# The samples' w_out tile in two passes, the samples' reads in two column groups, and another order of VectorE and loads behind the last head

## The chip, the cores and the metric

One core of one Trainium2 chip runs the program. The metric is the device time of one execution in microseconds, here the median of three runs: 1043.18 us (1041.35 to 1046.11).

## What is computed

One layer of a hybrid decoder for 1024 prompt tokens and 8 sample tokens (one new token for each of 8 sequences that have a past), with a final norm. Cut to what matters:

```python
def layer(x, ...):                       # x: prompt (1, 1024, 1024), samples (8, 1, 1024)
    z = rmsnorm(x, g_mix) @ w_in         # u | q | k | v | gate_a | gate_b
    pool_out, new_hist = pool_mixer(u, hist, ...)
    ret, s_new = retention(rotary(q), rotary(k), v, s0)     # 4 heads, 128 x 256 state
    mixed = sigmoid(ga) * pool_out + sigmoid(gb) * head_group_norm(ret, ret_gn)
    x = x + mixed @ w_out                # 1024 x 1024
    h2 = rmsnorm(x, g_ffn)
    x = x + hier_moe(h2, w_grp, w_exp, w1, w3, w2)          # 4 groups of 8 experts, top 2
    return x, new_hist, s_new
y = rmsnorm(x, g_final)                  # prompt and samples
```

For a sample, retention is one step for each head: the state is scaled and gets the outer product of key and value, and the query reads it.

## The kernel before

The work runs in stages: norm and transposition of x; four heads; stage C (w_out, second norm, router); the experts; the final norm. Every engine has its own program and they meet at counting semaphores (S["name"]). Each engine does its instructions in the written order, so that a wait holds up all that is written behind it.

**Precision.** Products with weights are made from a rounded part (hi) and the rest (lo) of both operands: hi by hi, hi by lo, lo by hi, in three passes. ScalarE writes hi, VectorE writes lo. The samples' projection in the heads puts hi and lo of the 8 tokens in different columns of one operand (hs) and takes two passes, one for each half of the weight; the partial results land in different rows and are added.

**Heads.** head(h) on TensorE makes nine products for u, q and k (n = 0 to 8, L1836), and between them the samples' part of the head before (attend_samples, L1775): grow(g) forms key by value for two samples, VectorE's update(h, g) (L2067) adds it to the states, read(g) (L1785) multiplies them with the queries. qm holds a query in one column of 32, a different one for each sample, so that all eight products add up in rows 96 to 127 (Q3:P) of one bank. Then follow eight chunks of 128 tokens and the samples as ninth (c = 8): project (v and gates), before (L1863: key transposed, scores of the next chunk), attend. VectorE's finish and finish_rest (L2032, L2053) normalise a chunk's output by head, with Newton steps for the root; GpSimd adds the pool part (L2248), raises sum_done and stores the rows to mixed_d. For the samples of head h-1 they run inside head h behind its products 6 and 7 (L2119, L2122). Behind these come the rotations of q and k, the pool means and scores(0), which writes scm.

**Last head into stage C.** In head 3 the raw w_out is split into hi and lo (low_wout for row blocks 0 to 2, low_wout_rest(i) for blocks 3, 4, 5 and then 6 with 7). TensorE mixes the samples' rest of head 3 with tile 0 of w_out (L947 to L958). VectorE's order is at L2196 to L2208 and L2217 to L2223, and below.

**Stage C.** Nine tiles t, eight of 128 tokens and the samples as tile 8 (CH). SyncE loads mixed rows and x (load_mixed, load_x); mixed_over(t) transposes them, high_mixed and low_mixed split them, out_product(t, ks) makes 48 products of 512 columns in row blocks k = 0 to 7. add_x(t) adds x. Within tile t the rest of tile t-1 is interleaved on TensorE: x2_over (transposes), router, count. VectorE does x2_second_half, norm, picks (group and experts of each token), places (slots in the experts' lists) for it. The loop is L959 to L976 on TensorE and L1201 to L1212 on VectorE. wo_used releases the first expert weights, which lie where w_out was.

```python
            dve.wait_ge(S["on_ready"], after(9 * H))
            dve.tensor_copy(count_b[:, :, :].rearrange("p a n -> p (a n)"), misc[:, BEFORE:BEFORE + 2 * P])
            for t in range(NT):
                if t == 1:
                    fold_router()
                if t > 0:
                    x2_second_half(t - 1)
                if t < CH:
                    low_mixed(dve, t + 1)
                if t > 0:
                    norm(t - 1)
                    picks(t - 1)
                    places(t - 1)
                add_x(t)
```

**SyncE.** tail(h, between) stores and loads the samples' states with other loads between (first_loads_c for the last head); behind its end stands head_stored, and then stage_c_sp, which begins with the four loads for the router (g_ffn in two forms, w_grp, w_exp) behind the last sum_done.

## Time and profile before

| | us |
|---|---|
| median of three runs | 1043.18 (1041.35 to 1046.11) |
| profiled execution, its own time | 1042.78 |
| its span, first to last instruction | 1041.0 |
| TensorE busy | 976.8 |
| VectorE busy | 737.1 |
| ScalarE busy | 443.0 |
| GpSimd busy | 219.0 |
| mean granted clock of TensorE | 0.978 |

PE is TensorE (PEld its loads of the stationary operand, which overlap with it), DVE VectorE, ACT ScalarE, POOL GpSimd, SP SyncE. Times in the rows are microseconds from the start of the span.
### The profile page before, as it was taken

The numbers are of one execution on the slowest core, as the hardware profiler recorded it, in microseconds if no ns is written. First come the engines' busy times: TensorE is split into PE (matmuls) and PEld (weight loads), VectorE is DVE, ScalarE is ACT, GpSimd is POOL, SyncE is SP. The second block draws the span as 40 slices with busy tenths as digits, with TensorE's granted clock in tenths as the row PEclk, the third lists the DMA queues.
The fourth block names the chain that finished last, engine by engine and source line by source line (L and its number), as shares of the span: only waits on it lengthen the run. The fifth ranks groups of instructions, "written<-read, shape, count | busy, mean of one in ns | idle before, by whom it ended". The sixth has DMA issues, their size and how long they took to land.

```text
span 1041.0 us, 16456 instructions
## 1 busy us (share of the span) xinstructions
PE 976.8 (94%) x5342; PEld 842.6 (81%) x5343; DVE 737.1 (71%) x1616; ACT 443.0 (43%) x738; POOL 219.0 (21%) x223
## 2 busy tenths in 40 slices
PE   5899999999999999999997999979999999999980
PEld 4898888988889888898885888857888888888860
DVE  4874556845558555684557555669999999999965
ACT  6622122121220121301112221136898889888974
POOL 0001220012200122011221000012444344443320
PEclk9999999999999999999999999989999999999995
DMA  9511115111151110511215433269999999999938
GB/s 290 195 31 62 31 32 170 31 62 31 32 160 42 30 62 22 173 38 42 71 56 207 170 147 123 103 245 376 388 395 399 390 392 395 394 392 384 361 55 331
DMA packets 74726, 190.23 MB, mean 183 GB/s; under 512 B 12503, under 2 KB 47555, under 8 KB 62227
## 3 DMA queue, kind: packets, MB, share of 16 engines
q1 hardware_dynamic: 61403, 159.66, 40.9%
q0 software_dynamic: 13248, 29.62, 9.8%
q8 instruction: 41, 0.67, 0.3%
q14 instruction: 34, 0.28, 0.1%
HBM read 167.43 MB, written 38.68 MB: 198 GB/s over the span
## 4 chain that ended last, share of the span: by engine, by line
PE 86%; DVE 5%; DMA 5%; issue 2%; ACT 1%; SPq 1%; POOL 0%; DVEq 0%; POOLq 0%; ACTq 0%
PE bank L1909 17%; PE bank L861 12%; PE bank L863 12%; PE bank L862 12%; PE bank L1910 9%; PE bank L892 9%; PE bank L1009 3%; PE bank L1898 1%; PE bank L922 1%; PE bank L1932 1%; PE bank L1924 1%; PE bank L1920 1%; PE bank L1789 1%; DMA raw<-in_w_in_dram 1%; PE bank L1928 1%
## 5 line engine op out<-in xcount | busy, mean ns | idle before, releaser
L1266 DVE TENSOR_TENSOR w_lo<-w,w_hi 128x1024 fp32r<-128x1024 f32 x128 | 150.5, 1217 | 0.2 <-DVE vec L1228 0.2
L750 ACT ACTIVATE w_hi<-w 128x1024 fp32r<-128x1024 f32 x128 | 129.7, 1068 | 3.0 <-PE bank L863 2.9
L1909 PE MATMUL bank<-wvg_hi,hT_hi 128*128 128x512 f32 x256 | 104.3, 407 | 0.0
L861 PE MATMUL bank<-w_hi,xT_hi 128*128 128x512 f32 x256 | 102.8, 402 | 1.3 <-issue 1.3
L1909 PE MATMUL bank<-wvg_lo,hT_hi 128*128 128x512 f32 x256 | 101.0, 395 | 0.0
L1909 PE MATMUL bank<-wvg_hi,hT_lo 128*128 128x512 f32 x256 | 100.7, 393 | 0.0
L863 PE MATMUL bank<-w_hi,xT_lo 128*128 128x512 f32 x256 | 100.2, 391 | 0.0
L862 PE MATMUL bank<-w_lo,xT_hi 128*128 128x512 f32 x256 | 99.8, 390 | 0.0
L1731 ACT ACTIVATE v<-bank 128x256 f32<-128x256 f32 x32 | 12.3, 383 | 201.2 <-PE bank L1910 201.2
L861 PE MATMUL bank<-hT_hi,wuqk_hi 128*128 128x344 f32 x288 | 95.6, 332 | 2.1 <-ACT line L1690 2.1
L2248 POOL TENSOR_TENSOR mixed<-onorm,pgate 128x256 f32<-128x256 f32 x36 | 39.2, 1088 | 276.0 <-DVE onorm L2065 276.0
L863 PE MATMUL bank<-hT_hi,wuqk_lo 128*128 128x344 f32 x288 | 93.3, 324 | 0.0
L862 PE MATMUL bank<-hT_lo,wuqk_hi 128*128 128x344 f32 x288 | 93.3, 324 | 0.0
L2165 DVE SCALAR_TENSOR_TENSOR state<-state,small,bank 128x256 f32<-128x256 f32 x28 | 13.5, 481 | 108.8 <-PE bank L1932 108.7
L1271 DVE TENSOR_TENSOR w_lo<-w,w_hi 128x1024 fp32r<-128x1024 f32 x62 | 73.2, 1222 | 15.7 <-ACT w_hi L758 15.7
L1448 POOL DMA_INDIRECT sum_d<-y,icol x28 | 45.5, 1624 | 133.3 <-ACT y L787 119.8
L1910 PE MATMUL bank<-wvg_hi,hT_hi 128*128 128x256 f32 x256 | 71.8, 280 | 0.0
L1910 PE MATMUL bank<-wvg_lo,hT_hi 128*128 128x256 f32 x256 | 71.7, 280 | 0.0
L1910 PE MATMUL bank<-wvg_hi,hT_lo 128*128 128x256 f32 x256 | 71.7, 280 | 0.0
L2237 POOL TENSOR_TENSOR sg<-sg,gn_b 128x256 f32<-128x256 f32 x36 | 26.6, 740 | 182.1 <-ACT sg L1733 178.2
L758 ACT ACTIVATE w_hi<-w 128x1024 fp32r<-128x1024 f32 x62 | 62.5, 1067 | 0.0
L861 PEld LDWEIGHTS bank<-hT_hi,wuqk_hi 128*128 128x128 f32 x288 | 55.2, 192 | 5.7 <-ACT line L1690 2.5
(262 smaller groups left out, 2388.4 us busy)
## 6 DMA issues: line engine op xcount, KB each, us to landing
w<-in_w_dram SPq DMA_DIRECT2D x96, 1024.0 KB, 17.4
raw<-in_w_in_dram SPq DMA_DIRECT2D x60, 256.0 KB, 3.2
xall<-in_x_prompt_dram SPq DMA_DIRECT2D x8, 512.0 KB, 7.9
mixed_d<-mixed POOLq DMA_DIRECT2D x32, 128.0 KB, 3.3
sample_state<-in_state_ret_dram SPq DMA_DIRECT2D x16, 256.0 KB, 3.6
out_dram<-sample_state SPq DMA_DIRECT2D x16, 256.0 KB, 4.0
mixed_in<-mixed_d SPq DMA_DIRECT2D x8, 512.0 KB, 4.3
x_again<-in_x_prompt_dram SPq DMA_DIRECT2D x8, 512.0 KB, 3.4
```

The costliest lines, as they stand in the source:

```text
L750: act.activation(hi, whole_w, ACT.Copy).then_inc(S["up_hi"], 1)
L758: act.activation(hi, whole_w, ACT.Copy).then_inc(S["down_hi"], 1)
L861: pe.matmul(out, lhs[0], rhs[0], start=first, stop=False)
L862: pe.matmul(out, lhs[0], rhs[1], start=False, stop=False)
L863: return pe.matmul(out, lhs[1], rhs[0], start=False, stop=last)
L892: mm = pe.matmul(banks[4 - 2 * s + n][:, :], mT[s][xi][:, k, :], wo[k][wi][:, n * 512:(n + 1) * 512], start=(k == 0 and xi + wi == 0), sto ...
L1266: dve.tensor_tensor(lo, whole_w, hi, ALU.subtract).then_inc(S["up_lo"], 1)
L1271: dve.tensor_tensor(lo, whole_w, hi, ALU.subtract).then_inc(S["down_lo"], 1)
L1448: pool.indirect_dma_start(out=sum_d, out_offset=bass.IndirectOffsetOnAxis(ap=index, axis=0), in_=yb[s2][:, :], in_offset=None, bounds_chec ...
L1909: g = pe.matmul(gates, x[xi], wvg[wi][:, 1:3, k, :], start=first, stop=last)
L1910: m = pe.matmul(v[:, 0:DV], x[xi], wvg[wi][:, 0, k, :], start=first, stop=last)
L2248: pool.tensor_tensor(mixed[s][:, :], onorm[:, :], pgate[:, :], ALU.add).then_inc(S["sum_done"], 1)
```

## The change

Samples' tile: sample_product takes its place. mT[0][0] holds hi in columns 0 to 7 and lo in columns 32 to 39 (low_samples), the products run with both halves of w_out, 32 in all, first for both halves of the 1024 output columns up to k = 4, then half 0 alone, then half 1. add_x_samples adds x and both row groups, half by half. Reads: the second product of each read goes to rows 64 to 95, and finish for the samples copies them and adds them to rows 96 to 127 before it goes on; finish_rest reads the sum from SBUF. VectorE: low_mixed(0), low_wout_rest(3), low_mixed(1) and add_x(0) stand earlier, finish and finish_rest for the last head's samples later, with waits for sum_done and head_stored behind them; places(0) and count(0) move into tile 2, places(7) behind add_x_samples. SyncE: the four router loads stand in the last head's tail, behind skv_mm. The transposition of gffn8 stands later in tile 1 and waits for pg_ready.

```diff
--- before.py
+++ after.py
@@ -403,7 +403,7 @@
 
         by_pe = {n: sem(n) for n in (
             "xt_mm", "g_col_mm", "uqk_mm", "g_mm", "v_mm", "kt_mm", "sc_mm", "o_mm", "kv_mm", "skv_mm", "so_mm",
-            "ht_mm", "ut_mm", "ct_mm", "w_mm", "wo_used", "t2_mm", "gf_mm", "l_mm", "count_mm", "list_mm",
+            "ht_mm", "ut_mm", "ct_mm", "w_mm", "w_half_mm", "wo_used", "t2_mm", "gf_mm", "l_mm", "count_mm", "list_mm",
             "spill_mm", "xt2_mm",
             "at_mm", "up_used", "down_used")}
         by_act = {n: sem(n) for n in (
@@ -637,16 +637,19 @@
                 load_x(sp, 0)
                 load_mixed(sp, 1)
             elif i == 3:
+                router_loads(sp)
                 load_mixed(sp, 2)
                 load_x(sp, 1)
 
-        def stage_c_sp(sp):
-            sp.wait_ge(S["sum_done"], after(9 * H))
+        def router_loads(sp):
+            sp.wait_ge(S["skv_mm"], after(4 * H))
             sp.dma_start(gffn_b[:, :], g_ffn[0:1, :].to_broadcast([P, D])).then_inc(route_in, 16)
             sp.dma_start(wr[:, :, 0:4], w_grp[0].rearrange("(k p) g -> p k g", p=P)).then_inc(route_in, 16)
             sp.dma_start(wr[:, :, 4:36], w_exp[0].rearrange("(k p) g e -> p k (g e)", p=P))\
                 .then_inc(route_in, 16)
             sp.dma_start(gffn8[0:KT, :], g_ffn[0].rearrange("(k p) -> k p", p=P)).then_inc(route_in, 16)
+
+        def stage_c_sp(sp):
             for t in range(2, CH + 1):
                 if t < CH:
                     load_mixed(sp, t + 1)
@@ -718,6 +721,8 @@
             def x2_first_half(t):
                 act.wait_ge(S["t2_mm"], after(2 * t + 1))
                 act.wait_ge(S["l_mm"], after(t - 1))
+                if t == 0:
+                    act.wait_ge(S["sgn_done"], after(9 * H))
                 m = columns(t)
                 act.activation(h2T[t % 2][:, 0:4, 0:m], banks[6][:, 0:4 * m].rearrange("p (k n) -> p k n", k=4), ACT.Copy)\
                     .then_inc(S["h2a_ev"], 1)
@@ -892,10 +897,20 @@
                             mm = pe.matmul(banks[4 - 2 * s + n][:, :], mT[s][xi][:, k, :],
                                            wo[k][wi][:, n * 512:(n + 1) * 512], start=(k == 0 and xi + wi == 0),
                                            stop=(k == KT - 1 and xi == 1))
-                    if t == CH and k in (2, 5):
-                        mm.then_inc(S["wo_used"], 1)
                 if ks[-1] == KT - 1:
                     mm.then_inc(S["w_mm"], 1)
+
+            def sample_product(ks, halves):
+
+                if ks[0] == 0:
+                    pe.wait_ge(S["m_lo"], after(2 * CH + 2))
+                    pe.wait_ge(S["x2_done"], after(2 * (CH - 1)))
+                for k in ks:
+                    for wi in range(2):
+                        for n in halves:
+                            mm = pe.matmul(banks[4 + n][:, :], mT[0][0][:, k, :], wo[k][wi][:, n * 512:(n + 1) * 512],
+                                           start=(k == 0 and wi == 0), stop=(k == KT - 1 and wi == 1))
+                return mm
 
             def x2_over(t, b):
 
@@ -956,24 +971,37 @@
             last_samples(5)
             last_samples(6)
             out_product(0, range(7, KT))
-            for t in range(1, NT):
-                if t < CH:
-                    mixed_over(pe, t + 1)
+            for t in range(1, CH):
+                mixed_over(pe, t + 1)
                 out_product(t, range(0, 1))
+                if t == 2:
+                    count(0)
                 x2_over(t - 1, 0)
+                out_product(t, range(1, 2))
+                x2_over(t - 1, 1)
                 if t == 1:
                     pe.wait_ge(route_in, 64)
+                    pe.wait_ge(S["pg_ready"], after(9 * H))
                     pe.transpose(banks[7][:, 0:KT], gffn8[0:KT, :], ident[0:KT, 0:KT]).then_inc(S["gf_mm"], 1)
-                out_product(t, range(1, 2))
-                x2_over(t - 1, 1)
                 out_product(t, range(2, 3))
                 router(t - 1)
                 out_product(t, range(3, 7))
-                count(t - 1)
-                if t == CH:
-                    for u in range(CH - 1):
-                        listing(u)
+                if t > 1:
+                    count(t - 1)
                 out_product(t, range(7, 8))
+            sample_product(range(0, 1), (0, 1))
+            x2_over(CH - 1, 0)
+            sample_product(range(1, 2), (0, 1))
+            x2_over(CH - 1, 1)
+            sample_product(range(2, 3), (0, 1)).then_inc(S["wo_used"], 1)
+            router(CH - 1)
+            sample_product(range(3, 5), (0, 1))
+            sample_product(range(5, KT), (0,)).then_inc(S["w_half_mm"], 1)
+            sample_product(range(5, 6), (1,)).then_inc(S["wo_used"], 1)
+            count(CH - 1)
+            for u in range(CH - 1):
+                listing(u)
+            sample_product(range(6, KT), (1,)).then_inc(S["w_mm"], 1)
             x2_over(CH, 0)
             x2_over(CH, 1)
             listing(CH - 1)
@@ -1091,7 +1119,16 @@
                                   mT[s][0][at].rearrange("p k n -> p (k n)"), ALU.subtract)\
                     .then_inc(S["m_lo"], 1)
 
-        def stage_c_dve(dve):
+        def low_samples(dve):
+
+            for b in range(2):
+                dve.wait_ge(S["m_hi"], after(2 * CH + b + 1))
+                own = mT[0][0][:, 4 * b:4 * b + 4, :]
+                turned_b = turned_mixed(CH, b).rearrange("p (k n) -> p k n", k=4)
+                dve.tensor_tensor(own[:, :, 32:32 + NB], turned_b[:, :, 0:NB], own[:, :, 0:NB], ALU.subtract)\
+                    .then_inc(S["m_lo"], 1)
+
+        def stage_c_dve(dve, finish_samples, finish_samples_rest):
             steps = Steps(dve, steps_c)
             do = steps.do
             rev4 = misc[:, REV + 4:REV + 8]
@@ -1196,20 +1233,44 @@
                     dve.tensor_tensor(x2[:, t, half], banks[4 - 2 * s + n][:, :], xr[s][:, half], ALU.add)\
                         .then_inc(S["x2_done"], 1)
 
-            dve.wait_ge(S["on_ready"], after(9 * H))
-            dve.tensor_copy(count_b[:, :, :].rearrange("p a n -> p (a n)"), misc[:, BEFORE:BEFORE + 2 * P])
-            for t in range(NT):
+            def add_x_samples(n):
+
+                dve.wait_ge(S["w_half_mm"] if n == 0 else S["w_mm"], after(1 if n == 0 else NT))
+                dve.wait_ge(xr_in[0], 16 * (CH // 2 + 1))
+                half = slice(n * 512, (n + 1) * 512)
+                do(dve.tensor_tensor(x2[:, CH, half], banks[4 + n][:, :], xr[0][:, half], ALU.add))
+                dve.tensor_tensor(x2[0:NB, CH, half], banks[4 + n][32:32 + NB, :], x2[0:NB, CH, half], ALU.add)\
+                    .then_inc(S["x2_done"], 1)
+
+            low_mixed(dve, 1)
+            add_x(0)
+            finish_samples()
+            for t in range(1, NT):
                 if t == 1:
                     fold_router()
-                if t > 0:
-                    x2_second_half(t - 1)
+                elif t == 2:
+                    places(0)
+                x2_second_half(t - 1)
+                if t == 1:
+                    finish_samples_rest()
+                    dve.wait_ge(S["on_ready"], after(9 * H))
+                    dve.wait_ge(S["sum_done"], after(9 * H))
+                    dve.wait_ge(S["head_stored"], after(H))
+                    dve.tensor_copy(count_b[:, :, :].rearrange("p a n -> p (a n)"), misc[:, BEFORE:BEFORE + 2 * P])
+                if t < CH - 1:
+                    low_mixed(dve, t + 1)
+                elif t < CH:
+                    low_samples(dve)
+                norm(t - 1)
+                picks(t - 1)
                 if t < CH:
-                    low_mixed(dve, t + 1)
-                if t > 0:
-                    norm(t - 1)
-                    picks(t - 1)
+                    if t > 1:
+                        places(t - 1)
+                    add_x(t)
+                else:
+                    add_x_samples(0)
+                    add_x_samples(1)
                     places(t - 1)
-                add_x(t)
             x2_second_half(CH)
             norm(CH)
             picks(CH)
@@ -1772,6 +1833,9 @@
                             if t % 3 == 2 if g < 2 else t == 7:
                                 mm.then_inc(S["xt_mm"], 1)
 
+            def quarter(i):
+                return slice(Q3, P) if i == 0 else slice(64, Q3)
+
             def attend_samples(h, n):
 
 
@@ -1786,8 +1850,8 @@
                     pe.wait_ge(S["s_upd"], after(4 * h + g + 1))
                     for i in range(2):
                         b = 2 * g + i
-                        mm = pe.matmul(sample_bank(h)[Q3:P, 0:DV], qm[:, b, :], sst[g % 2][:, i, :],
-                                       start=(b == 0), stop=(b == NB - 1))
+                        mm = pe.matmul(sample_bank(h)[quarter(i), 0:DV], qm[:, b, :], sst[g % 2][:, i, :],
+                                       start=(g == 0), stop=(g == NB // 2 - 1))
                     mm.then_inc(S["so_mm"], 1)
 
                 if n == 1:
@@ -2027,7 +2091,7 @@
                 elif n > 2:
                     for q in ((7, 8, 9), (10, 11, 12, 13, 14, 15), (16, 17))[n - 3]:
                         low_first(q)
-            per_head, per_tail = 104, 5 + NEWTON
+            per_head, per_tail = 106, 7 + NEWTON
 
             def finish(h, c):
 
@@ -2041,6 +2105,12 @@
                 dve.wait_ge(S["sum_done"], after(9 * h + c))
                 bank = banks[6] if c < CH else sample_bank(h)
                 o = bank[r, 0:DV]
+                if c == CH:
+                    steps.do(dve.tensor_copy(onorm[r, :], bank[64:Q3, 0:DV]))
+                    carried(dve, "dve")
+                    steps.do(dve.tensor_tensor(onorm[r, :], o, onorm[r, :], ALU.add))
+                    carried(dve, "dve")
+                    o = onorm[r, :]
                 dve.tensor_tensor(pgate[r, :], bank[r, DV:2 * DV], sg[s][r, 0:DV], ALU.mult)\
                     .then_inc(S["pg_ready"], 1)
                 steps.do(dve.bn_stats(small[r, STAT:STAT + 6], o))
@@ -2054,7 +2124,7 @@
 
                 r = slice(0 if c < CH else Q3, P)
                 s = c % 2
-                o = (banks[6] if c < CH else sample_bank(h))[r, 0:DV]
+                o = banks[6][r, 0:DV] if c < CH else onorm[r, :]
                 newton_rsqrt(steps, dve, small[r, HALF:HALF + 1], small[r, GUESS:GUESS + 1],
                              small[r, TMP:TMP + 1]).then_inc(S["rstd_done"], 1)
                 dve.wait_ge(S["rstd_done"], after(9 * h + c + 1))
@@ -2189,6 +2259,8 @@
                         dve.wait_ge(S["v_ev"], after(9 * h + 9))
                         dve.tensor_tensor(vs[0:32, :], banks[2][64:Q3, 0:DV], vs[64:Q3, :], ALU.subtract)\
                             .then_inc(S["kblk_done"], 1)
+                        if last:
+                            low_mixed(dve, 0)
                         dve.wait_ge(S["g_mm"], after(9 * h + 9))
                         steps.do(dve.tensor_copy(sg[0][Q3:P, :], banks[1][64:Q3, :]))
                         dve.tensor_tensor(sg[0][Q3:P, :], sg[0][Q3:P, :], banks[1][Q3:P, :], ALU.add)\
@@ -2196,7 +2268,6 @@
                     if c > 0:
                         grow_state(c - 1)
                         if c == CH and last:
-                            low_mixed(dve, 0)
                             sample_queries()
                             update(h, 0)
                             update(h, 1)
@@ -2215,12 +2286,10 @@
             steps.round_(before_heads - per_tail, H, per_head)
 
             low_wout_rest(dve, 2)
+            low_wout_rest(dve, 3)
             update(H - 1, 2)
             update(H - 1, 3)
-            low_wout_rest(dve, 3)
-            finish(H - 1, CH)
-            finish_rest(H - 1, CH)
-            stage_c_dve(dve)
+            stage_c_dve(dve, lambda: finish(H - 1, CH), lambda: finish_rest(H - 1, CH))
 
 
         @block.gpsimd
```

## Rows read from the trace of the kernel before

**Rows 1.** Page: span, busy time by engine, and who ends the chain.

```profile
span 1041.0 us, 16456 instructions
...
PE 976.8 (94%) x5342; PEld 842.6 (81%) x5343; DVE 737.1 (71%) x1616; ACT 443.0 (43%) x738; POOL 219.0 (21%) x223
...
PE 86%; DVE 5%; DMA 5%; issue 2%; ACT 1%; SPq 1%; POOL 0%; DVEq 0%; POOLq 0%; ACTq 0%
```

**Rows 2.** Waits of TensorE: who waited for whom, total, times, longest (us).

```profile
PE bank L876 <- DVE mT_lo L1090: 4.1, 1, 4.1
...
PE bank L892 <- issue: 1.4, 1, 1.4
```

**Rows 3.** Timeline of TensorE: start, us, line, operation, tiles, idle time before.

```profile
548.00 0.70 PE L892 MATMUL bank<-wo_hi,mT_hi 128*128 128x512 f32 x2 [1.44 <-issue]
...
558.24 1.03 PE L876 MATMUL bank<-misc,mixed_in 128*128 128x128 f32 x8
...
562.69 1.91 PE L1789 MATMUL bank<-sample_state,qm 128*32 128x256 f32 x8
...
570.28 1.40 PE L876 MATMUL bank<-misc,mixed_in 128*128 128x128 f32 x8 [4.07 <-DVE mT_lo L1090]
...
587.47 1.03 PE L876 MATMUL bank<-misc,mixed_in 128*128 128x128 f32 x8
...
602.19 1.03 PE L876 MATMUL bank<-misc,mixed_in 128*128 128x128 f32 x8
```

**Rows 4.** Windows: span, busy of PE, PEld, DVE, ACT, POOL, clock, DMA, GB/s.

```profile
572.00:574.00 2.00, 2.00 (x6) 1.46 (x5) 0.00 (x0) 0.00 (x0) 0.00 (x0) 0.50 1.00 203
```

**Rows 5.** Timeline of VectorE, 525 to 720, behind the last head's projection.

```profile
544.77 0.69 DVE L2193 COPY sg<-bank 32x512 f32<-32x512 f32 x1
...
546.62 1.28 DVE L1090 TENSOR_TENSOR mT_lo<-bank,mT_hi 128x512 fp32r<-128x512 f32 x2
...
556.10 1.22 DVE L495 TENSOR_TENSOR wo_lo<-wo_raw,wo_hi 128x1024 fp32r<-128x1024 f32 x1
558.47 1.45 DVE L2070 SCALAR_TENSOR_TENSOR sample_state<-sample_state,small,bank 128x512 f32<-128x512 f32 x2 [1.16 <-DMA sample_state<-in_state_ret_dram]
...
564.64 0.43 DVE L2044 TENSOR_TENSOR pgate<-bank,sg 32x256 f32<-32x256 f32 x1 [2.46 <-PE bank L1789]
```

**Rows 6.** Timeline of ScalarE, 536 to 600: high half of tile 0's operand.

```profile
544.31 1.09 ACT L714 ACTIVATE mT_hi<-bank 128x512 fp32r<-128x512 f32 x2
```

**Rows 7.** Timeline of the SyncE queue, 535 to 760: router loads and tile 3.

```profile
570.26 0.35 SPq L645 DMA_DIRECT2D gffn_b<-in_g_ffn_dram  x1
...
573.52 0.54 SPq L614 DMA_DIRECT2D mixed_in<-mixed_d  x1
```

**Rows 8.** Tile mixed_in, window 573.4 to 574.1: landing of that one load (us).

```profile
DMA to landing us min/median/max: 3.7/3.7/3.7
```

**Rows 9.** Source view of line 1789, the reads: duration in ns min/median/max.

```profile
L1789 PEld LDWEIGHTS bank<-sample_state,qm x64: 106/110/110, 164.4 to 564.0; 128*32 128x32 f32 x64
L1789 PE MATMUL bank<-sample_state,qm x64: 379/379/403, 164.6 to 564.2; 128*32 128x256 f32 x64
```

**Rows 10.** Timeline of VectorE in heads 1 (first two rows) and 3.

```profile
188.32 0.18 DVE L2048 BATCH_NORM_AGGREGATE small<-small 32x2 f32<-32x6 f32 x1 [0.16 <-DVE small L2046]
...
205.26 0.29 DVE L2130 TENSOR_TENSOR scm<-bank,hc 128x128 f32<-128x128 f32 x1
...
467.61 0.28 DVE L2130 TENSOR_TENSOR scm<-bank,hc 128x128 f32<-128x128 f32 x1
```

**Rows 11.** Timeline of TensorE, heads 1 and 3: scores of chunk 1.

```profile
205.87 0.39 PE L1876 MATMUL bank<-qT,kT 128*128 128x128 f32 x2
...
469.01 0.39 PE L1876 MATMUL bank<-qT,kT 128*128 128x128 f32 x2
```

**Rows 12.** Chain of waits, 670 to 705: start, us, what.

```profile
682.64 5.57 PE bank L892 x24
...
690.46 0.70 DVE x L1196
```

## The prediction

> **What bounds the kernel now.** The page comes first. TensorE is busy for 976.8 of 1041.0 us and ends 86% of the chain [rows 1], so the time is TensorE's work plus the holes in it, and a step is worth only what it takes out of TensorE's stream. I then read the waits of TensorE. Beside the start and the end, two holes lie where the change is: 4.1 us for VectorE's low half of a mixed tile and 1.4 us ahead of the first w_out product [rows 2]. The timeline of TensorE places them at 546.56 to 548.00 and at 566.21 to 570.28 [rows 3]. Behind the longer one the granted clock is 0.50 [rows 4], that is 1.2 instead of 2.4 GHz, so this hole costs more than its length. Tile 1's period runs from 566.21 to 587.47, 21.26 us, tile 2's from there to 602.19, 14.72 us [rows 3]. The difference of 6.5 us is the hole, the low clock, and a short wait for gffn8.
>
> **1. VectorE's order behind the last head.** Before, low_mixed(0) starts at 546.62, behind both gate sums, which start at 544.77, and the state [rows 5]. Its input is there when ScalarE's pair, begun at 544.31 and 1.09 us long, is through, at 545.40 [rows 6]. Moved ahead of the sums it runs some 0.2 us idle included, to about 546.25, while TensorE is free at 546.56: the 1.44 us hole goes. Next late is VectorE. Everything from the sums to finish_rest of chunk 7 is the same work in another order, so it ends some 0.3 us later, and the low half of w_out row block 5, at 556.10 before [rows 5], starts near 556.4 and ends near 557.6. TensorE reaches that block at about 557.4 (558.24 plus 0.8 for the transposes, less the 1.44 and some 0.2): a hole of 0.2. Blocks 6 and 7 now follow at once (1.2 us each), to 560.0, then two updates of 0.7 each (1.45 for the pair [rows 5]) to 561.4. The samples' states must have landed; before they landed at 558.47 [rows 5], now near 559.7, since their queue starts about 1 us later: covered, by 0.3 only. TensorE's last reads wait for these updates, end near 562.2, and block 7 (1.4 us) ends tile 0 near 563.8 instead of 566.2. That is **2.4 us**.
>
> Then VectorE does low_mixed(1) right away, to about 562.6, where it was behind the samples' 14 small steps that begin at 564.64 [rows 5]. The 4.07 us hole and its low clock go; finish for the samples moves behind add_x(0), its rest and a wait for GpSimd's sum behind x2_second_half(0). Queued behind it on VectorE are low_mixed(2), norm(0), picks(0) and add_x(1). I lay them out from their durations on the same timeline: finish_rest ends near 573.9, GpSimd's sum 0.8 later, low_mixed(2) near 576.3, picks(0) near 581.5, add_x(1) near 582.9. TensorE wants low_mixed(2) at 580, the count at 582.1 and add_x(1)'s first half at 582.2. It fits because count(0) and places(0) moved one tile on; the cost is 0.1 us. The wait for head_stored is open from near 568 (stores issued near 562 and 5.9 us to land), 6 us ahead of its use.
>
> **2. SyncE's queue.** The four router loads leave it near 557.4 instead of 570.26, ahead of load_mixed(2), load_x(1), the last two state stores and head_stored. They hold the queue for 3.3 us (570.26 to 573.52 [rows 7]). The short wait for gffn8 goes. But tile 2's mixed rows, so far issued in front of all four, are now issued near 560.7 and needed at 563.8. The case before that is nearest is tile 3's load, right behind the same four loads: issued at 573.52 [rows 7], landed 3.7 us later [rows 8], so 7.0 us after the first router load. That gives 564.4 here, and up to 1.3 us more because the states' 512 KB stand in front. Floor: no hole. Ceiling: 2.5 us. I take 1.3. Such a hole is about as long as the one at 546.56, behind which TensorE's pairs kept their pace (0.70 us for the first, as for others [rows 3]), so no low clock.
>
> Tile 1 then costs its 14.72 and about 0.2: 563.8 + 1.3 + 14.8 = 579.9 instead of 587.47. Parts 1 and 2 together give **7.5 us**, from 6.3 (ceiling) to 8.8 (floor).
>
> **3. The samples' w_out tile in two passes.** 48 products become 32. One costs 5.57/24 = 0.232 us [rows 12], so 3.7 us go, all on the path. The two passes put the high and the low part in different columns of one operand; the loads of the operand stay one a product. VectorE must follow. picks(7) starts when router(7) is done, 1.4 us earlier than before, and the count behind half 0 comes later than the picks; add_x_samples(0) then runs under half 1. Behind the last product stand, as before, two additions (0.70 us for the first, at 690.46 [rows 12]), now with a wait of 0.16 [rows 10] between them. places(7) falls into the time in which ScalarE takes the mean and the root, and nearly fills it. Gain **3.4 us**, from 2.6 (places(7) late by 0.8) to 3.7. The expert weights' first loads are released 1.4 and 1.9 us earlier; nothing waits for them there.
>
> **4. The reads in two column groups.** A read is four passes of one column group, 0.22 us apart: eight passes take 1.91 us, of which the last is 0.38 [rows 3, 9]. Now the order is A, A, B, B: the passes of one product stay in one group and in order, so at best the second A runs beside the first B. With its operand's load, 110 ns [rows 9], begun when the second A starts, B can start 0.11 us behind instead of 0.22. Gain a read: 0 (no overlap), 0.11, or 0.22 (load fetched earlier too). The trace has no two groups in flight; I take 0.11, the row of the load. Only the twelve reads in heads 1 to 3 count, since in the last head the updates set the pace: 1.3 us, from 0 to 2.6.
>
> The Trainium skill, "TensorE: Matmul & The Clock Gate", part 3 (packing small matmuls), says that matmuls in different column groups start about 4 ns apart and gives 2.38 times for three of them. By that rule a read would fall by half, by 0.43 us; the same part says that matmuls keep program order, which speaks against it for pairs of passes. No row of before shows which holds.
>
> **5. What the two groups cost VectorE.** finish for the samples gets a copy and an addition, each about 0.43 us and a wait of 0.16 [rows 5, 10]: 1.2 us. In heads 1 to 3 this stands in an unbroken run of VectorE that starts with TensorE's product 6 and ends in scm(0). TensorE's scores of chunk 1 wait for scm(0). In head 1 it ends at 205.55 and they start at 205.87: slack 0.32 [rows 10, 11]; head 2 has the same. In head 3 it is 467.89 against 469.01, slack 1.1. So 1.2 - 0.3 = 0.9 us a head is lost in heads 1 and 2 and 0.1 in head 3, less 0.1 to 0.2 a head because normalising from SBUF instead of PSUM may be shorter. The gain of part 4 does not help here: it lies ahead of product 6. Cost **1.5 us**, from 0.8 to 2.0.
>
> **Sum.** 7.5 + 3.4 + 1.3 - 1.5 = 10.7 us. The profiled run took 1042.8 us (1.8 around its span of 1041.0), which gives 1032.1; the median of the three runs is 0.4 higher, so 1032.5.
>
> **Rivals.**
> (a) The reads do not overlap at all: the change's second item does nothing but cost. 1032.5 + 1.3 = 1033.8. For it: VectorE's slack is real and overlap unseen.
> (b) They overlap more: both passes of one product run beside the other's, two passes' time saved, 0.43 us for each of twelve reads: 5.2 instead of 1.3, so 1028.6; with one pass, 0.22, 1031.2. Against: the order of the passes. It is what the Trainium skill's packing section leads to.
> (c) Tile 2's rows come so late that the hole is about as long as the old one of 4.07: 2.8 us more, and some 2 us of low clock as then: 1037.3. For it: the states, the router loads and the mixed rows share the engines. Against: the 3.7 us landing [rows 8].
> (d) Slower: VectorE now waits for head_stored with low_mixed(2) to add_x(1) behind it. From 574.7 on every us that the last state stores are late stops TensorE by one, plus low clock. The gain is eaten when it comes at about 583, 21 us behind its stores instead of 5.9; landing at 590 would give 1032.5 + 15.3 + 2 = 1049.8. Against: nothing else fills the queues then.
> (e) VectorE's delay at the tail or in the tiles costs 3 us more than laid out, without a low clock: 1035.5.
>
> **How the numbers follow.** Forecast (part 4 at 0.11, the rest as summed) 0.45; (a) 0.22; (b) 0.13, both its forms; (c) 0.09; (e) 0.09; (d) 0.02. The range must leave out at most 0.2: from 1028.5, which holds (b), to 1036.5, which holds (a) and (e) and leaves (c) and (d) out. A measurement here can tell about 0.5%, 5.2 us, so the bounds of "same" are 1038.0 and 1048.4. Only (d) lies beyond; part of (c), if its stall grows, and mishaps of (e)'s kind reach into "same": faster 0.93, same 0.05, slower 0.02.
>
> **What would show it.** No wait of TensorE over 2.5 us between 545 and 700, and a full clock there; the start of tile 2's period (the fourth block of eight transposes of mixed rows) 7.5 us earlier than 587.47, apart from the heads' shift; a hole of 0.5 to 2 us ahead of tile 2's transposes, put down to a DMA; 32 products for the samples and their last one about 11 us earlier in all; scores of chunk 1 in heads 1 and 2 waiting 0.7 to 0.9 us for scm; in the reads, the third pass starting 0.11 behind the second. The prediction is wrong if the hole before tile 2's transposes is over 3 us, if VectorE's run in the heads has slack that I did not see, or if picks(7) ends behind half 0 of the samples.

## The result, and the profile after

The changed kernel takes 1035.02 us in the median (1033.34 to 1037.92, 4 runs) beside 1042.88 us (1041.35 to 1046.11, 4 runs) of the kernel before: ratio 0.9921, 95% interval 0.9901 to 0.9940. It is faster by 7.9 us; 10.7 were forecast. The profiled execution took 1037.92 us, the slowest of its four. Its page: span, busy time by engine, who ends the chain.

```profile
span 1036.2 us, 16450 instructions
...
PE 969.0 (94%) x5326; PEld 836.8 (81%) x5327; DVE 740.0 (71%) x1626; ACT 442.7 (43%) x738; POOL 218.1 (21%) x223
...
PE 83%; DMA 6%; DVE 6%; issue 2%; ACT 2%; SPq 1%; DVEq 0%; POOL 0%; POOLq 0%; ACTq 0%
```

Against [rows 1] TensorE is busy 7.8 us less, but the span is only 4.8 us shorter, and DMA, VectorE and ScalarE end more of the chain. So some of what was taken out of TensorE's stream came back as waits. The ones read below are, in order of their total (who waited for whom, us, times, longest):

```profile
PE bank L881 <- DMA mixed_in<-mixed_d: 3.8, 1, 3.8
PE bank L866 <- ACT line L1751: 3.5, 3, 2.6
...
PE bank L1037 <- DMA xg<-h_d,idx_tok: 1.0, 1, 1.0
PE bank L1973 <- DVE kT L2181: 0.9, 2, 0.5
```

The waits of [rows 2] for mT_lo and for issue ahead of the first w_out product are gone. In their place stands a hole ahead of the transposes of tile 2's mixed rows (L881), and three smaller waits that I had not put into the sum; the one for ScalarE's line (L866) was there before too, with 2.1 us. TensorE's timeline shows where the first one is:

```profile
545.33 0.63 PE L897 MATMUL bank<-wo_hi,mT_hi 128*128 128x512 f32 x2
...
550.95 0.63 PE L1853 MATMUL bank<-sample_state,qm 128*32 128x256 f32 x4
...
560.09 0.63 PE L1853 MATMUL bank<-sample_state,qm 128*32 128x256 f32 x4 [0.16 <-DVE sample_state L2140]
560.89 0.63 PE L1853 MATMUL bank<-sample_state,qm 128*32 128x256 f32 x4 [0.17 <-DVE sample_state L2140]
...
566.94 1.20 PE L881 MATMUL bank<-misc,mixed_in 128*128 128x128 f32 x8 [3.84 <-DMA mixed_in<-mixed_d]
567.79 1.20 PE L897 MATMUL bank<-wo_hi,mT_hi 128*128 128x512 f32 x2
568.79 1.05 PE L897 MATMUL bank<-wo_lo,mT_hi 128*128 128x512 f32 x2
```

The first product starts without a hole. Four passes of a read take 0.63 us. The hole is 3.84 us long, and behind it a pair of w_out passes takes 1.05 to 1.20 us instead of 0.63; the windows' clock (third figure from the right) confirms the lower level, 1.2 GHz:

```profile
567.00:569.00 2.00, 2.00 (x11) 1.81 (x12) 0.28 (x2) 0.00 (x0) 0.00 (x0) 0.70 0.98 326
569.00:571.00 2.00, 2.00 (x7) 1.50 (x7) 0.00 (x0) 0.00 (x0) 0.00 (x0) 0.50 0.15 51
```

For all later comparisons I cut every trace at the same points of TensorE's stream. This table is worked out from starts of products. h1 to h3 u: from the first u product of heads 1, 2, 3 to their first product for v, added up (here lie the reads). Chunks: the rest of these three heads. Tile 0: from its mixed transposes to its end. Tile 1: from there to the fourth block of mixed transposes. Tiles 2 to 6: the next five periods, to the ninth block of mixed transposes. Tiles 7, 8: from there to the last w_out product (tile 8 is the samples' tile; tile 7 is the same in all rows, so that the differences are those of the samples' tile). Gather: from there to the first expert's transposes. Experts 1, 2: the first two periods of the experts. End: from the last expert's transposes to the end of the span.

| kernel | h1 to h3 u | chunks | tile 0 | tile 1 | tiles 2 to 6 | tiles 7, 8 | gather | experts 1, 2 | end | span |
|---|---|---|---|---|---|---|---|---|---|---|
| before | 125.9 | 265.4 | 22.7 | 21.4 | 73.6 | 29.0 | 14.9 | 8.5, 8.6 | 46.1 | 1041.0 |
| after | 124.0 | 265.9 | 20.7 | 20.7 | 73.7 | 25.6 | 16.0 | 10.1, 7.7 | 46.7 | 1036.2 |
| a0_after | 124.4 | 265.9 | 20.5 | 17.8 | 73.6 | 25.6 | 16.0 | 8.5, 8.6 | 47.3 | 1033.7 |
| e1_mixed_first | 123.0 | 266.0 | 20.5 | 15.1 | 73.6 | 25.6 | 16.1 | 8.5, 8.5 | 47.7 | 1028.9 |
| b1_mixed_first | 122.6 | 266.0 | 20.5 | 15.0 | 73.6 | 25.6 | 16.0 | 8.5, 8.6 | 46.7 | 1027.5 |
| e2_one_group | 125.7 | 265.4 | 20.5 | 20.7 | 73.6 | 25.6 | 16.0 | 10.1, 7.7 | 47.1 | 1037.8 |
| e3_three_passes | 123.6 | 266.0 | 22.2 | 19.6 | 73.6 | 29.0 | 14.3 | 8.5, 8.6 | 46.2 | 1037.2 |
| e4_no_sum | 122.2 | 265.4 | 21.3 | 18.6 | 73.6 | 25.6 | 16.0 | 8.5, 8.5 | 47.3 | 1032.8 |
| e5_scores_first | 124.4 | 265.4 | 20.5 | 15.0 | 73.6 | 25.6 | 16.1 | 8.5, 8.5 | 47.5 | 1030.7 |
| e6_hold_second | 123.4 | 266.0 | 20.5 | 16.0 | 73.6 | 25.6 | 18.5 | 11.3, 7.7 | 46.8 | 1033.3 |
| e7_all | 119.8 | 265.4 | 20.5 | 15.3 | 73.6 | 25.6 | 18.7 | 11.5, 7.7 | 46.7 | 1029.7 |
| e8_best | 119.7 | 265.4 | 21.5 | 15.0 | 73.6 | 25.6 | 16.0 | 11.0, 7.7 | 47.3 | 1028.4 |

How far two profiles of one kernel differ can be read from it: after and a0_after are the same kernel, and so are e1 and b1. Tile 1 differs by 2.8 us and the first two experts by 0.7 where the low clock comes in one of them, the end by 1.0, the heads by 0.5; the rest is level within 0.2. Between different kernels tile 0 moves as well, from 20.5 to 22.2, for reasons told under part 1.

### The profile page after: what moved, and what is told of

It reads as the page before. It is cut to its first block, busy times and chain, and to the rows that moved or that the text cites. A ratio compares the mean times of both kernels' runs of the same rounds, so it can differ in the third digit from the quotient of the medians.

```text
span 1036.2 us, 16450 instructions
## 1 busy us (share of the span) xinstructions
PE 969.0 (94%) x5326; PEld 836.8 (81%) x5327; DVE 740.0 (71%) x1626; ACT 442.7 (43%) x738; POOL 218.1 (21%) x223
## 4 chain that ended last, share of the span: by engine, by line
PE 83%; DMA 6%; DVE 6%; issue 2%; ACT 2%; SPq 1%; DVEq 0%; POOL 0%; POOLq 0%; ACTq 0%
PE bank L1973 17%; PE bank L866 11%; PE bank L868 11%; PE bank L867 11%; PE bank L1974 9%; PE bank L897 8%; PE bank L1037 3%; DMA raw<-in_w_in_dram 2%; PE bank L1962 1%; PE bank L937 1%; PE bank L1988 1%; PE bank L1996 1%; PE bank L1984 1%; DVE x L1449 1%; PE bank L1992 1%
## 5 line engine op out<-in xcount | busy, mean ns | idle before, releaser
L866 PE MATMUL bank<-w_hi,xT_hi 128*128 128x512 f32 x256 | 103.6, 405 | 1.8 <-issue 1.8
L1973 PE MATMUL bank<-wvg_hi,hT_hi 128*128 128x512 f32 x256 | 104.3, 407 | 0.9 <-DVE kT L2181 0.9
L1973 PE MATMUL bank<-wvg_lo,hT_hi 128*128 128x512 f32 x256 | 101.0, 394 | 0.0
L1973 PE MATMUL bank<-wvg_hi,hT_lo 128*128 128x512 f32 x256 | 100.6, 393 | 0.0
L866 PE MATMUL bank<-hT_hi,wuqk_hi 128*128 128x344 f32 x288 | 95.5, 332 | 3.5 <-ACT line L1751 3.5
L866 PEld LDWEIGHTS bank<-hT_hi,wuqk_hi 128*128 128x128 f32 x288 | 55.2, 192 | 7.0 <-ACT line L1751 4.1
```

What stands on the lines that cost most here:

```text
L866: pe.matmul(out, lhs[0], rhs[0], start=first, stop=False)
L1973: g = pe.matmul(gates, x[xi], wvg[wi][:, 1:3, k, :], start=first, stop=last)
```

## The experiments

**The kernel after, again,** on the chip of the first three experiments.

> The changed kernel as it is, once more, as the measure for the others of this group. Its profiled run of before this was the slowest of four (1037.9 against 1033.3 to 1035.1), so I expect a ratio to the kernel before of 0.9915 to 0.993 and a span near 1033. If the 3.84 us hole ahead of tile 2's transposes is the rule, it stands here again at 3 to 4 us with low clock behind it; if it belonged to that one run, it is 0.5 to 2 us, as I forecast, and the granted clock stays full.

Measured 1035.01 us (1032.14 to 1038.50), ratio 0.9925 [0.9901, 0.9949]. In its profile the hole ahead of tile 2 is 2.6 us, and the clock stays up. The four router loads hold SyncE's queue for 4.2 us here (557.61 to 561.77), and in after, as shown next, for 5.5.

**e1: the router loads behind tile 2's rows.**

```diff
             elif i == 3:
-                router_loads(sp)
                 load_mixed(sp, 2)
                 load_x(sp, 1)
+                router_loads(sp)
```

> The four router loads behind load_mixed(2) and load_x(1), all else as changed. Theory (SyncE's queue is what made tile 2's rows late: 5.5 us in front of them): the rows are issued near 557.5, the hole ahead of tile 2's transposes and the low clock behind it go, and the kernel gains 4 us of hole and 1.5 to 2 us of clock less what comes late next, 4 to 6 us against the changed kernel. Rival (the transfers of the router weights in small pieces fill the DMA engines, whatever the order of issue): the hole moves to the wait for gffn8 or to the mixed rows again, and the gain is under 2 us.

Measured 1031.55 us, 0.9899 [0.9880, 0.9919], 3.5 us faster than a0_after in the median, somewhat less than the 4 to 6 expected, and later on another chip:

> The kernel of e1_mixed_first again, on the same chip as e8_best, to stand beside it. Every theory: ratio 0.988 to 0.992. The hole ahead of tile 2's transposes is absent (all of the theory that the router loads held up tile 2's rows), tile 1 takes about 15.1 us. Theory 1 of e8 says that this run's u parts of heads 1 to 3 together are some 3 to 4 us longer than e8's; theory 2 says that they are level within 1.5 us. For the end stretch (last residual addition to the end): if it was chance, it lands anywhere between 46 and 47.7 us in both; if it comes from the order, both show the same value within 0.3.

Measured 1029.42 us, 0.9878 [0.9855, 0.9901]. SyncE's queue tells what happened. First after, then e1 (start, time in which the queue is held, line, transfer):

```profile
557.52 0.46 SPq L646 DMA_DIRECT2D gffn_b<-in_g_ffn_dram  x1
558.02 0.43 SPq L647 DMA_DIRECT2D w_router<-in_w_grp_dram  x1
558.50 1.19 SPq L648 DMA_DIRECT2D w_router<-in_w_exp_dram  x1
559.73 3.16 SPq L650 DMA_DIRECT2D gffn<-in_g_ffn_dram  x1
563.00 0.34 SPq L614 DMA_DIRECT2D mixed_in<-mixed_d  x1
```

```profile
554.98 0.40 SPq L614 DMA_DIRECT2D mixed_in<-mixed_d  x1
...
555.91 0.42 SPq L646 DMA_DIRECT2D gffn_b<-in_g_ffn_dram  x1
556.38 0.43 SPq L647 DMA_DIRECT2D w_router<-in_w_grp_dram  x1
556.85 3.39 SPq L648 DMA_DIRECT2D w_router<-in_w_exp_dram  x1
560.28 3.08 SPq L650 DMA_DIRECT2D gffn<-in_g_ffn_dram  x1
```

In after the four loads hold the queue for 5.5 us (557.52 to 563.00), where [rows 7] gave 3.3. Tile 2's rows are issued at 563.00 and TensorE, which was free at 563.10, starts on them at 566.94. In e1 they leave first, at 554.98; the same four loads then hold the queue even longer, 7.5 us, and nobody waits for it, since gffn8 and the router's weights are wanted later. In after the rows, once issued, are there within 3.9 us. So their late issue made the hole, and not, as the rival had it, the transfers of the router's weights ahead of them. TensorE passes from tile 0 into tile 1 without a hole:

```profile
560.29 0.62 PE L897 MATMUL bank<-wo_hi,mT_lo 128*128 128x512 f32 x2
560.75 1.06 PE L881 MATMUL bank<-misc,mixed_in 128*128 128x128 f32 x8
```

Tile 1 costs 15.0 to 15.1 us in both profiles. It is shown that the place of the router loads costs tile 1 2.8 us (a0) to 5.6 us (after). Both are worked out from the table. In after the tile's work, from its first transposes on, takes 16.7 us (566.94 to 583.59), in e1 15.1 (560.75 to 575.82): of the 5.6, 1.6 are the low clock and 4.0 lie ahead of these transposes, 3.84 of them idle. The margin of the new order is small: in e6, which has it too, TensorE waits 0.7 us for these rows, issued at 555.05 and wanted at 561.02.

**e2: the reads of heads 0 to 2 back in one group,** without VectorE's copy and addition.

```diff
-                        mm = pe.matmul(sample_bank(h)[quarter(i), 0:DV], qm[:, b, :], sst[g % 2][:, i, :],
-                                       start=(g == 0), stop=(g == NB // 2 - 1))
+                        two = h == H - 1
+                        mm = pe.matmul(sample_bank(h)[quarter(i if two else 0), 0:DV], qm[:, b, :], sst[g % 2][:, i, :],
+                                       start=(g == 0 if two else b == 0),
+                                       stop=(g == NB // 2 - 1 if two else b == NB - 1))
...
-                if c == CH:
+                if c == CH and isinstance(h, int) and h == H - 1:
...
```

> In heads 0 to 2 the samples' reads go back to one column group and finish for them back to no copy and addition; the last head's keep two groups. Theory from the new trace (four passes of a read now take two slots, 0.43 us saved each, of which TensorE gives back 0.9 us a head in waits for ScalarE's u and VectorE's k, and 0.25 in the scores): about 1.4 to 1.7 us slower than the changed kernel, and the waits for ScalarE's line and VectorE's kT in heads 1 to 3 gone. Rival (forecast: 0.11 a read, and VectorE's 0.9 a head lost): the same time within 0.5 us, or faster by up to 0.5.

Measured 1037.18 us, 0.9944 [0.9928, 0.9961], so 2.2 us slower than a0_after in the median, where 1.4 to 1.7 were expected. The intervals overlap; what carries the reading is the table. u parts and chunks return to the values of before within 0.2 us (125.7 and 265.4), while the seven profiles that have two groups and both of VectorE's new steps (after, a0, e1, b1, e3, e5, e6) have 122.6 to 124.4, mean 123.6 beside 125.7 here. The two groups are a gain of 2.1 us less 0.6 in the chunks, 1.5 net. One wait for ScalarE's line stays (1.9 us), as in the kernel before (2.1).

**e4: two groups, but without the copy and the addition in heads 0 to 2.** It leaves the second product of each of these reads (rows 64 to 95) out of the samples' output.

```diff
-                if c == CH:
+                if c == CH and isinstance(h, int) and h == H - 1:
                     steps.do(dve.tensor_copy(onorm[r, :], bank[64:Q3, 0:DV]))
...
```

> The changed kernel with two column groups in all reads, but without finish's copy and addition for the samples of heads 0 to 2: the second product of each read (rows 64 to 95) is left out of those samples' output. Theory (VectorE's 1.2 us in each of heads 1 to 3 is what TensorE waits for at k's rotation, 0.45 us twice, and at scm(0), 0.2 us twice): both waits gone, 1.1 to 1.4 us faster than the changed kernel, and the wait for ScalarE's line stays at two times 0.8 to 1.1. Forecast (0.9 us lost in heads 1 and 2, 0.1 in head 3): 1.8 us faster. Rival (TensorE, 1.2 us early, meets another wait): under 0.5 us.

Measured 1033.21 us, 0.9901 [0.9879, 0.9922], 1.8 us faster than a0_after in the median. The chunks are back at 265.4 and TensorE has no wait for kT (L1973, the first product for v and the gates) any more; the u parts are 122.2, 1.4 below the mean of the seven and 0.4 below the lowest of them.

**e5: e1, and scores(0) ahead of the last two steps of the pool means on VectorE.**

```diff
                                                head_tab(h, 2 * P, 16), ALU.mult))
+                    between()
                     steps.do(dve.scalar_tensor_tensor(
...
-                        pool_means()
+                        pool_means(lambda: scores(0))
...
```

> e1_mixed_first with scores(0) ahead of the last two steps of the pool means. Theory: only the scores' share of VectorE's delay goes, 0.2 us in each of heads 1 and 2, since TensorE has been held up at k's rotation before it: 0.3 to 0.5 us faster than e1_mixed_first in the heads' stretches of the trace, which the medians cannot tell. If the forecast's size were right, 1.5 us faster.

Measured 1030.93 us, 0.9876 [0.9855, 0.9897]. The chunks are at 265.4, so the 0.6 us there are the scores' wait for scm; the waits for kT (0.9 us) stay, because the rotation of k stands ahead of the pool means on VectorE. e4 and e5 together show VectorE's price: 0.6 through the scores, and 0.9 through the waits for kT, which come with the two new steps (e2 and e4 are without them); 1.5 in all. The 0.9 is read from the rows of these waits; the u parts scatter too much to show it.

**e3: the samples' tile again with 48 products,** in three passes, without the second addition.

```diff
-                    for wi in range(2):
+                    for xi, wi in ((0, 0), (0, 1), (1, 0)):
                         for n in halves:
-                            mm = pe.matmul(banks[4 + n][:, :], mT[0][0][:, k, :], wo[k][wi][:, n * 512:(n + 1) * 512],
-                                           start=(k == 0 and wi == 0), stop=(k == KT - 1 and wi == 1))
+                            mm = pe.matmul(banks[4 + n][:, :], mT[0][xi][:, k, :], wo[k][wi][:, n * 512:(n + 1) * 512],
+                                           start=(k == 0 and xi + wi == 0), stop=(k == KT - 1 and xi == 1))
...
-                    low_samples(dve)
+                    low_mixed(dve, CH)
```

> The samples' w_out tile again with 48 products and its full low half, but in the new order by halves. Theory (all 16 products lie on the path): 3.7 us slower, less 0.2 for the second additions that go: 3.2 to 3.7 us. Rival (the gain is lost behind it, because the gather of the first expert's rows and the first expert weights then come last, as 1.1 us more between the last product and the first expert's transposes in the new trace hints): 2 to 2.7 us slower.

Measured 1037.84 us, 0.9942 [0.9924, 0.9960], 2.8 us slower than a0_after in the median. Tiles 7 and 8 take 29.0 us again, 3.4 more, but the way from the last product to the first expert is 14.3 instead of 16.0 us (14.9 before): a third (against before) to a half (against e3) of what the shorter tile gains is lost behind it. GpSimd shows where. First after, then e3: the store of the samples' h2 rows, and the first gather, which waits for it.

```profile
688.66 0.52 POOL L1467 DMA_DIRECT2D h_d<-h  x1 [9.57 <-DVE h L1158]
...
695.10 1.38 POOL L1492 DMA_INDIRECT xg<-h_d,idx_tok  x1 [5.42 <-DMA h_d<-h]
```

```profile
691.85 0.52 POOL L1466 DMA_DIRECT2D h_d<-h  x1 [11.45 <-DVE h L1158]
...
697.50 1.10 POOL L1491 DMA_INDIRECT xg<-h_d,idx_tok  x1 [4.63 <-DVEq L1282]
```

From the last w_out product to the store after takes 5.8 us and e3 5.1: the second addition behind the last product (0.68 us) is not there in e3. From store to gather after takes 6.44 us and e3 5.65; in the kernel before it was 5.66:

```profile
695.76 0.52 POOL L1406 DMA_DIRECT2D h_d<-h  x1 [12.10 <-DVE h L1121]
...
701.42 1.10 POOL L1431 DMA_INDIRECT xg<-h_d,idx_tok  x1 [4.64 <-DMA h_d<-h]
```

The first expert weights (five transfers, the first issued at 675.93 in after, at 680.96 before) keep the DMA engines full until some 18 us after that issue, in both: the share of after is still 0.90 in the window 692 to 694, where the store of 688.66 is under way, and 0.04 in the next:

```profile
692.00:694.00 2.00, 1.43 (x8) 1.26 (x9) 1.34 (x8) 0.00 (x0) 0.00 (x0) 0.50 0.90 373
```

Since the tile is shorter but the weights still take 18 us, the store meets them for longer: it lands 4.8 us behind its issue before, 4.6 in e3, and in after later:

```profile
DMA to landing us min/median/max: 5.6/5.6/5.6
```

The 0.8 us from store to gather are this. The gather has a second condition, the list of tokens: in e3 the profile names VectorE's signal that it is done (L1282) and not the store, which had landed 1.1 us before the gather began.

**e6: e1, with the second release of expert weights held back until the samples' rows are stored.**

```diff
                     sp.wait_ge(S["wo_used"], after(b + 1))
+                    if not is_first(b, 1):
+                        sp.wait_ge(h2_out[0], 16 * 5)
```

> e1_mixed_first, and the second release of expert weights (3 MB) waits until the samples' h2 rows are stored. Theory (in the changed kernel these rows land only when 5 MB of weights have, 18 us after the first release, which came only 1.4 to 2 us earlier, so the gather of the first expert's rows is late by 1 us): from the last list product to the first expert's transposes 5.3 us again instead of 6.3 to 6.4, 1 us faster in the trace. Rival (the gather then shares the engines with the held weights): no gain, or up to 2 us slower because the second expert's weights come late.

Measured 1034.78 us, 0.9919 [0.9898, 0.9939], 3.2 us slower than e1 in the median and 3.9 slower than e5.

```profile
681.83 0.52 POOL L1469 DMA_DIRECT2D h_d<-h  x1 [9.56 <-DVE h L1160]
...
687.47 1.10 POOL L1494 DMA_INDIRECT xg<-h_d,idx_tok  x1 [4.62 <-DVEq L1285]
```

```profile
PE bank L1039 <- DMA xg<-h_d,idx_tok: 4.4, 1, 4.4
```

The store's landing in e6:

```profile
DMA to landing us min/median/max: 2.1/2.1/2.1
```

In e1 it takes 5.4 us. That confirms the reading of e3: with fewer weights in flight the store lands sooner, here by 3.3 us. Yet from store to gather it is 5.64 instead of 6.24 us, only 0.6 less, because the gather then waits for the list (DVEq L1285), as in e3; the store can't give more than that. And the weights now meet the gathers: the first gathered rows land 7.0 us behind their issue instead of 4.0, TensorE waits 4.4 us for them instead of 1.8 in e1, and the first expert runs at the low clock (11.3 us instead of 8.5). The remedy is worse than the fault.

**e7: e6 and e5 together, and ScalarE's evictions of u for n = 1 and 2 ahead of the three weight pieces behind which they stood.** rounds(n) does the three pieces.

```diff
                     else:
-                        for q in range(6 + 3 * n, 9 + 3 * n):
-                            round_piece(act, q, h, None)
+                        if n == 0:
+                            rounds(n)
...
                             .then_inc(S["u_ev"], 1)
+                    if n > 0 and not first:
+                        rounds(n)
```

> e1_mixed_first with both of the above, and in heads 1 to 3 ScalarE moves u of parts 1 and 2 out of its bank ahead of the three weight pieces of that part instead of behind them. Theory (reads in two groups save 0.43 us each, 1.7 us a head, and 0.9 to 1.1 us of it is lost to u being late behind pieces whose loads are late): the two waits for ScalarE's line in heads 1 and 2 go, 1.5 to 2 us; with the others 2.5 to 3.5 us faster than e1_mixed_first, a ratio near 0.987. Rival (VectorE's k is next late and takes it all): 1 us or less.

Measured 1030.75 us, 0.9872 [0.9850, 0.9894], 4.0 us faster than e6, which holds the release too; against e1 it is 0.8, where 2.5 to 3.5 were expected: the stretches that the hold lengthens (gather, experts 1 and 2) take 4.8 us more than in e1. The u parts fall from 123.6 to 119.8 us, and no wait for ScalarE's line is left. The reason is seen on ScalarE in head 1. First a0_after, then e8, which has the same ScalarE order as e7:

```profile
164.41 0.63 ACT L1674 ACTIVATE wvg_hi<-raw 128x512 fp32r<-128x512 f32 x1 [1.19 <-DMA raw<-in_w_in_dram]
166.04 0.63 ACT L1674 ACTIVATE wvg_hi<-raw 128x512 fp32r<-128x512 f32 x1 [1.00 <-DMA raw<-in_w_in_dram]
166.58 0.44 ACT L1751 ACTIVATE line<-bank 128x344 f32<-128x344 f32 x1
```

```profile
160.95 0.46 ACT L1755 ACTIVATE line<-bank 128x344 f32<-128x344 f32 x1 [3.64 <-PE bank L868]
162.58 0.63 ACT L1674 ACTIVATE wvg_hi<-raw 128x512 fp32r<-128x512 f32 x1 [1.18 <-DMA raw<-in_w_in_dram]
```

In a0_after the eviction of a u bank stands behind pieces that wait for their weight loads; TensorE needs that bank, and waits for it:

```profile
167.07 0.43 PE L866 MATMUL bank<-hT_hi,wuqk_hi 128*128 128x344 f32 x1 [1.10 <-ACT line L1751]
```

In the kernel before the same product starts at 165.96 without a wait; it had one wait of this kind in a later head:

```profile
PE bank L861 <- ACT line L1690: 2.1, 1, 2.1
```

So TensorE, faster through the reads, only ran into ScalarE's queue, whose pace the weight loads set. With the eviction ahead of the pieces the read's saving comes through: 12 reads by 0.43 are 5.2 us, the old wait of 2.1 us for ScalarE goes too, and 0.9 for kT come on: 6.4 worked out, 6.0 measured (125.9 to 119.8). How the 6.0 divide is worked out and not measured: no run has ScalarE's new order with one column group.

**e8: e7 without the held release.**

> e7_all without the edit that held back the second release of expert weights; it keeps the router loads behind tile 2's rows, scores(0) ahead of the last two steps of pool_means, and ScalarE's evictions of u ahead of the three weight pieces. Theory 1 (the hold cost what e6 showed against e1: last w_out product to first expert's transposes 18.5 to 18.7 instead of 16.1 us, first expert 11.4 instead of 8.5 us at a low clock, 0.8 us given back by the second expert): the first two return to 16.1 and 8.5, and the kernel is about 4 us faster than e7, near 1026.5, ratio about 0.984 against the kernel before; u parts of heads 1 to 3 together stay near 120 us. Theory 2 (the stretches of the heads vary by themselves and the ScalarE order did little): the u parts come back to near 124 us, and the kernel stands level with e5, near 1030.9, ratio 0.9875.

Measured 1030.05 us (1025.77 to 1031.25), 0.9860 [0.9836, 0.9885]: the lowest ratio of all, and its interval lies wholly below that of a0_after. The u parts are 119.7 beside 122.6 of b1 on the same chip, and the gather is back at 16.0: theory 1 for these two. It failed for the first expert, which stays at the low clock (11.0 us), and the median is 3.5 us above the 1026.5 that I gave. Between the medians of e8 and b1 (1030.05 and 1029.42) there is no difference that counts; e8's heads 1 to 3 are 3.5 us shorter in the profile, and the start with head 0, tile 0, the first two experts and the end take 4.3 us more. I can't say why the clock falls at the first expert. TensorE was busy for about half of the time in the windows ahead of it both in after, where it fell (1.05 and 1.03 of 2 us), and in a0_after, where it didn't (0.93 and 0.99); first after, then a0_after, the second of these windows and the one with the clock of the expert's first products:

```profile
699.00:701.00 2.00, 1.03 (x8) 0.84 (x8) 0.76 (x2) 1.08 (x2) 1.70 (x2) 0.98 0.79 234
701.00:703.00 2.00, 1.96 (x5) 1.61 (x6) 1.79 (x10) 0.00 (x0) 1.15 (x3) 0.50 1.01 418
```

```profile
697.00:699.00 2.00, 0.99 (x7) 0.73 (x7) 1.35 (x4) 1.09 (x2) 1.62 (x3) 1.00 0.91 336
699.00:701.00 2.00, 2.00 (x10) 1.66 (x9) 1.70 (x11) 0.83 (x1) 1.02 (x1) 1.00 0.97 406
```

## Why the prediction was right, and where its sum was wrong

The time lies in the range, 2.5 us above the forecast. That is owed in part to luck and to a range of 8 us: 2.9 us in tile 1 did not come, 1.1 behind the samples' tile and 1.3 elsewhere were lost, and the heads, where two terms were wrong, gave 1.3 more than forecast. Term by term, gains in us, measured as the mean of the two profiles of the changed kernel against the one of before:

| | forecast | measured | with the cause removed |
|---|---|---|---|
| tile 0 (part 1) | 2.4 | 2.1 | |
| tile 1 (parts 1 and 2) | 5.1 | 0.8 and 3.6, mean 2.2 | 6.4 (e1, b1) |
| samples' tile (part 3) | 3.4 | 3.4 | |
| behind it, to the first expert | 0 | -1.1 | |
| first two experts | 0 | -0.7 and 0, mean -0.3 | |
| reads and their cost in heads 1 to 3 (parts 4, 5) | -0.2 | 1.1 | 6.2 (e8) |
| tiles 2 to 6 | 0 | -0.1 | |
| start with head 0, other experts, end | 0 | -1.3 | |
| sum | 10.7 | 6.0 | |

The spans differ by 6.0 in these profiles and the medians by 7.3 and 7.9; single profiles scatter that much, as the table of stages shows.

**Part 1 was right.** The hole at 546.56 is gone, tile 0 gains 2.1 of 2.4, and the states' updates are as tight as laid out: TensorE's last reads wait 0.16 and 0.17 us in after (0.44 and 0.84 in e3, 1.01 in e8, where the states land later: the cover of 0.3 was too thin). VectorE's order in the tiles held, since tiles 2 to 6 cost 73.7 us beside 73.6. Rival (d), the wait for head_stored, is seen in no trace.

One thing that I had not laid out limits tile 0 now: tile 1's mixed rows. Before, they landed at 555.0 and were wanted at 558.24. In after TensorE is through with w_out's block 4 at 554.78 and sits idle until the rows, issued at 548.09, have landed at 555.7. The profile names no releaser here, but in every profile of the changed kernel and its variants TensorE starts 0.1 us behind that landing.

```profile
555.74 1.06 PE L881 MATMUL bank<-misc,mixed_in 128*128 128x128 f32 x8 [0.96 <-issue]
```

```profile
DMA to landing us min/median/max: 7.6/7.6/7.6
```

This hole is 0.2 us in b1 and 1.9 in e3, and with the states' landing it is why tile 0 takes 20.5 to 22.2 us.

**Part 2 failed at one number.** The step was "They hold the queue for 3.3 us", read from one place in a quiet stretch, and carried to another place where state stores and loads were in flight (that these are what slows the issue is an inference; no run takes them away). The issue of the router loads began where I had put it (557.52, forecast near 557.4), but held the queue for 5.5 us (4.2 in a0, 5.7 in e2). Tile 2's rows thus left at 563.00 instead of 560.7 and landed 3.9 us later at the latest, close to the 3.7 of [rows 8]. The hole was 2.6 to 3.9 us in the profiles with this order, not 1.3, with a ceiling of 2.5 that I had believed: rival (c) in its mechanism, to which I gave 0.09, though its 1037.3 us did not come. By the prediction's own sign, a hole over 3 us, it was wrong here in after, e2 and e4, and not in a0 and e3. My second step there, that such a hole leaves the clock alone, is settled neither way: holes of 2.6 (a0) and 3.4 us (e4) left it up, 2.8 (e3), 3.8 (after) and 3.9 us (e2) were followed by the low clock. So its length by itself does not decide it here.

**Part 3's own term was right and its cover was not.** 3.39 us against 3.4. "Nothing waits for them there" failed: the expert weights have nobody waiting, but the small store of the samples' rows is under way together with them and lands 0.8 us later than before, and the gather that waits for it takes 0.3 us longer: that is the 1.1 us.

**Parts 4 and 5.** The step "the passes of one product stay in one group and in order, so at best the second A runs beside the first B" was wrong. With two groups the passes pair up, A1 with B1, A2 with B2. The timeline of after shows it also for another pair of products, wp,ps beside a product of a read: starts 0.01 us apart, and the second passes 0.24 us behind, 0.01 apart.

```profile
549.54 0.40 PE L1868 MATMUL bank<-wp,ps 128*32 128x256 f32 x1
549.55 0.40 PE L1853 MATMUL bank<-sample_state,qm 128*32 128x256 f32 x1
549.78 0.38 PE L1868 MATMUL bank<-wp,ps 128*32 128x256 f32 x1
549.79 0.80 PE L1853 MATMUL bank<-sample_state,qm 128*32 128x256 f32 x3
```

This pair shows more. wp,ps writes rows 96 to 127, as the first product of the read does, so what runs beside it must be the read's second product (rows 64 to 95), which the program has written last. In the trace the increment of so_mm, which the program puts behind that second product, indeed stands on the pass of 549.79, and two passes of the read follow it:

```profile
L1853 PE MATMUL bank<-sample_state,qm x2: 379/379/379, 550.0 to 550.2; 128*32 128x256 f32 x2
```

So a product whose column group was free has passed one whose group was taken, in the first read of all four heads, and the count so_mm says nothing of the other product there.

A read of four passes takes 0.63 us where one group takes 1.03, as in e2's row:

```profile
165.09 1.03 PE L1854 MATMUL bank<-sample_state,qm 128*32 128x256 f32 x4
```

That is rival (b) in its larger form. The Trainium skill, "TensorE: Matmul & The Clock Gate", part 3 (packing small matmuls), gives starts about 4 ns apart in different column groups; the rows agree to their 0.01 us. Its statement that matmuls keep program order, which I had held against the pairs, does not hold in this trace: not for the passes of a pair, and not for the two products of these first reads.

But rival (b)'s price, 5.2 us, did not come either, because TensorE was not the only one that set the pace of the u parts. ScalarE's evictions behind weight pieces and VectorE's kT took back all but about 2 us, and e7 and e8 show that with the first of them moved the whole saving arrives. Part 5's size was right by sum, 1.5 forecast and 1.5 measured, but 0.9 of it came through the first products for v, which wait for the rotation of k (L1973), and only 0.6 through the scores. A forecast of -0.2 and a measured 1.1 to 1.5 look close; two wrong terms stand behind that.

**What stays open.** Why the first expert falls to the low clock in some kernels. And why the end takes 46.1 us before and 46.2 in e3 but 46.7 to 47.7 in all others: e1 and b1, one kernel, differ by 1.0, so most of it is scatter, but no other run came as low as these two.

## What to carry to other kernels

Moving a load costs its queue the time of issue at the new place, and this time is not that of the old place: put what is needed next in front, and the rest, however long it holds the queue, behind. A faster engine gains only what its neighbours let through: before costing a shorter product at its full worth, look at who evicts its banks and what stands ahead of that eviction. And a transfer released earlier without anybody waiting for it still meets the small stores behind it. Where products in different column groups follow each other, the count behind the last one written does not tell that the others are through.
